# Second norm stage: diagonals of inverse roots made by ScalarE from the identity, VectorE keeps the inverses

## The reference

```
def rms_norm(x, w):
    xf = x.astype(jnp.float32)
    y = xf * lax.rsqrt(jnp.mean(xf * xf, axis=-1, keepdims=True) + EPS)
    return (y * w.astype(jnp.float32)).astype(x.dtype)

def finish(x, y_gla, y_nsa, w_out, norm_mix_post, norm_ffn_pre, norm_ffn_post, w_ff_up, w_ff_down):
    y = jnp.concatenate([y_gla, y_nsa], axis=-1) @ w_out
    x = x + rms_norm(y, norm_mix_post)
    h = rms_norm(x, norm_ffn_pre)
    u = jnp.square(jax.nn.relu(h @ w_ff_up))
    return x + rms_norm(u @ w_ff_down, norm_ffn_post)
```

## Time and profile before

| what | value |
|---|---|
| time, median of 3 runs | 2026.84 us (2023.39 to 2028.88) |
| profiled execution | 2025.4 us, span of its trace 2023.6 us |
| TensorE busy | 1906.8 us (94%) |
| VectorE busy | 689.9 us (34%) |
| GpSimd busy | 547.8 us (27%) |
| ScalarE busy | 519.2 us (26%) |
| second norm stage, in the trace | from 1158.4 us to 1212.1 us |

### The profile page before, as it was taken

How to read it: one execution, slowest core, us unless ns; L and a number is a source line. 1 busy time by engine, 2 the same in 40 slices (tenths; PEclk the granted TensorE clock), 3 DMA queues, 4 the chain that set the end, 5 groups by cost and what they waited for, 6 DMA issues and landing times. The chain is left out here.

```text
span 2023.6 us, 26094 instructions
## 1 busy us (share of the span) xinstructions
PE 1906.8 (94%) x10662; PEld 1550.7 (77%) x10662; DVE 689.9 (34%) x1555; ACT 519.2 (26%) x1169; POOL 547.8 (27%) x458
## 2 busy tenths in 40 slices
PE   7999999879999699999969969999999999999996
PEld 6888887745556487777758768888888888888885
DVE  5321213567665233424230175300332133213323
ACT  3311212377677334334221140010000010000002
POOL 3212222157664221111112143222222222222124
PEclk9999999889999799999969979999999999999998
DMA  4111122120000675656423100111111111111112
GB/s 134 32 52 52 55 51 63 61 89 1 1 1 1 228 239 178 222 181 235 133 60 115 25 21 22 55 48 42 42 42 42 42 42 42 42 42 42 42 53 84
DMA packets 113630, 149.73 MB, mean 74 GB/s; under 512 B 21584, under 2 KB 99320, under 8 KB 105256
## 3 DMA queue, kind: packets, MB, share of 16 engines
q1 hardware_dynamic: 104296, 80.95, 13.3%
q0 software_dynamic: 9216, 67.11, 9.9%
HBM read 139.96 MB, written 12.27 MB: 75 GB/s over the span
## 5 line engine op out<-in xcount | busy, mean ns | idle before, releaser
L278 PE MATMUL PS<-Z,ring 128*128 128x258 f32 x1152 | 258.2, 380 | 0.0
L1816 PE MATMUL PS<-Z 128*128 128x256 f32 (+1 forms) x1024 | 244.6, 385 | 0.0
L278 PEld LDWEIGHTS PS<-Z,ring 128*128 128x128 f32 x1152 | 218.1, 189 | 33.0
L278 PE MATMUL PS<-hT,ring 128*128 128x258 f32 x992 | 226.9, 386 | 7.6 <-DMA ring<-in_w_out 7.0
L1816 PEld LDWEIGHTS PS<-Z 128*128 128x128 f32 x1024 | 186.5, 190 | 42.8 <-issue 20.3
L278 PEld LDWEIGHTS PS<-hT,ring 128*128 128x128 f32 x992 | 190.4, 193 | 37.6 <-DMA ring<-in_w_out 7.1
L2362 ACT ACTIVATE Z<-PS 128x516 f32<-128x516 f32 x80 | 48.1, 601 | 646.9 <-PE PS L278 646.9
L241 POOL TENSOR_TENSOR Z<-ring 128x512 f32<-128x512 f32 x36 | 46.7, 1298 | 604.5 <-PE PS L278 533.5
L278 PE MATMUL PS<-Z 128*128 128x258 f32 x832 | 187.1, 380 | 0.0
L278 PEld LDWEIGHTS PS<-Z 128*128 128x128 f32 x832 | 157.5, 189 | 23.9
L2382 DVE TENSOR_TENSOR Z<-PS,Z 128x516 f32<-128x516 f32 x96 | 66.8, 695 | 314.9 <-PE PS L278 314.9
(11 more groups left out here) (379 smaller groups left out, 2736.7 us busy)
## 6 DMA issues: line engine op xcount, KB each, us to landing
ring<-in_w_ff_up SPq DMA_DIRECT2D x32, 512.0 KB, 5.3
ring<-in_w_ff_down SPq DMA_DIRECT2D x32, 512.0 KB, 4.2
ring<-in_w_in SPq DMA_DIRECT2D x9, 1024.0 KB, 5.0
X<-in_x_prompt SPq DMA_DIRECT2D x8, 1024.0 KB, 11.2
srow<-in_state_nsa_win SPq DMA_DIRECT2D x16, 256.0 KB, 5.3
out_y_prompt<-X SPq DMA_DIRECT2D x8, 512.0 KB
out_win_sample<-in_state_nsa_win SPq DMA_DIRECT2D x1, 4088.0 KB
out_kv_prompt<-Z SPq DMA_DIRECT2D x8, 256.0 KB, 2.0
```

The costliest lines, as they stand in the source:

```text
L278: last = nc.tensor.matmul(M.PS[:, bank_of(M, n, e) + c, 0:CW], a[:, k, :], b[:, k, c * CW:(c + 1) * CW], start=e in (M1, M2, M5) and k == ...
L1816: last = nc.tensor.matmul(out, w1s[:, v, half, 2 * r + e, :], x2[seg][:, r, v, :, e, half:half + SEG[seg]], start=(j == 0), stop=(j == 15))
```

## The change

In the second norm stage (front and back both there) VectorE's `diagonal` now only inverts the root and signals it under a new semaphore, "back_inverse". ScalarE gets a `diagonal` of its own: an ACTIVATE with the function Copy that reads the identity with the inverse root as its scale, and signals "diag_ready". It stands at the start of ScalarE's turn t for tile t - 3, ahead of the square of tile t, and waits for the inverse and, from tile 2 on, for the matmuls of tile t - 2 that read the same buffer. The loop of ScalarE becomes one turn longer. The first and the third norm stage stay as they were.

```
-    rta, rtb = M.sem("front_root"), M.sem("back_root")
+    rta, rtb, invb = M.sem("front_root"), M.sem("back_root"), M.sem("back_inverse")
...
         @block.scalar
         def _(act):
-            for t in range(NT + LAG):
+            def diagonal(t):
+                n = toks(t)
+                act.wait_ge(invb, t + 1)
+                if t >= 2:
+                    act.wait_ge(bkd, b0 + t - 1)
+                nc.scalar.activation(diag[0:n, t % 2, 0:n], M.ident[0:n, 0:n], ACT.Copy, scale=st[0:n, 3, t:t + 1])\
+                  .then_inc(dgr, 1)
+
+            for t in range(NT + PLAG):
+                if front is not None and back is not None and t >= PLAG:
+                    diagonal(t - PLAG)
                 if front is not None and t < NT:
...
-                if back is not None and t >= LAG:
+                if back is not None and LAG <= t < NT + LAG:
...
             def diagonal(t):
                 n = toks(t)
                 dve.wait_ge(rtb, b0 + t + 1)
+                if front is not None:
+                    r = st[0:n, 3, t:t + 1]
+                    nc.vector.reciprocal(r, r).then_inc(invb, 1)
+                    return
                 inverse(t, 2)
```

## The result

| | before | after |
|---|---|---|
| time, median of 4 runs | 2026.63 us (2023.39 to 2028.88) | 2012.31 us (2010.51 to 2014.37) |
| profiled execution, span | 2025.4, 2023.6 us | 2013.24, 2011.5 us |
| second norm stage in the trace | 1158.42 to 1212.05, 53.63 us | 1160.41 to 1199.86, 39.45 us |
| trace behind the stage | 811.55 us | 811.64 us |

The changed kernel is faster: ratio 0.9927, 95% interval 0.9915 to 0.9939, 14.3 us of the medians. The stage is 14.2 us shorter. The spans differ by only 12.1 us, because the stretch ahead of the stage, which the change doesn't touch, took 2.0 us longer in this execution.

A forecast was written before the change was run, and what follows sets the result against it. The prediction took VectorE's move, late behind diagonals held by GpSimd's adds, to bound the second norm stage. Two turns and end piece: 37.35 us before, 14.6 + 10.2 = 24.8 after, gain 12.5, so 2014.3 us, range 2009.5 to 2021.5.

The forecast's parts named there:

- What bounds the stage: Second norm stage: TensorE waits 12.9 us for VectorE's move into hT, late because diagonals of 1649 ns each stand ahead.
- the hold: VectorE's diagonal waits on SBUF ports until GpSimd's add ends: 2.40 us instead of 0.29, 10.9 us over the stage.
- ScalarE's price: Cost of one diagonal as a ScalarE ACTIVATE: 0.39 us, bounded by 0.29 undisturbed and 2.40 if held by the add.
- The turn: Two tiles, from one scaling to the scaling two tiles on: 12.24 us before, 7.29 forecast; two turns 23.53 to 14.6.
- The second ring: ScalarE's and VectorE's chain of waits per tile: 3.35 us, 6.7 a turn, costing nothing until the diagonal passes about 0.7.
- the ring through the move: Chain of scaling, reciprocal, move, matmuls, transposes, square and root back to a scaling: forecast 7.29 us a turn.
- The end piece: From the scaling of tile 8 to the last move: 13.82 us before, forecast 10.2, between 8.6 and 11.8.
- Ahead of tile 4: Stage before the scaling of tile 4: no change, plus or minus 0.7 us, as VectorE's first diagonals met adds only briefly.
- The start of the feed-forward stage: Clock there may be low for longer or shorter than now: no change, plus or minus 1.7 us.
- Rival 1: TensorE's clock stays low: two turns 20.6 us, end 11.8, a gain of 4.9, 2022 us; chance 0.10.
- Rival 2: VectorE's move is held until the add's end instead of the diagonal: gain near 0, 2027 us; chance 0.05.
- Rival 3: ScalarE switches tables, two loads of 1.283 us per diagonal: 2034 us; chance 0.03, shared with a held ScalarE.

The follow-up runs named there:

- e1: Kernel before, VectorE's diagonals in the second norm stage made in the tensor_scalar form that also writes a sum: 2017.55 us, ratio 0.9947.
- e4: Changed kernel, VectorE's move in turns 4 to 8 also waiting for GpSimd's add of the same turn: 2025.75 us, ratio 0.9992.
- e9: Changed kernel with VectorE's move of tile t - 4 at the start of its turn, ahead of the scaling: 2008.82 us (one execution).
- e5: Changed kernel with each of ScalarE's diagonals made twice, the extra one into an unused place: 2014.19 us (one execution).
- e6: Changed kernel with each of ScalarE's diagonals made four times, the extra ones into an unused place: 2019.32 us (one execution).
- e2: Kernel before with VectorE's move of tile t - 4 put ahead of the reciprocal and diagonal of tile t - 2: 2012.26 us (one execution).
- e3: Kernel before with each of GpSimd's adds in the second norm stage made in two halves of 512 columns: 2012.85 us (one execution).
- e8: e7 with VectorE's move of tile t - 5 at the very start of its turn, ahead of the scaling: 2009.13 us, again 2007.44 us.
- e7: Changed kernel with the back half a turn later, move ahead of the reciprocal, ScalarE's diagonal after the front's root: 2009.61 us, ratio 0.9910.

## Why the prediction was right

- **What bounds the stage.** Right, and shown from both sides: e1 takes the hold away and leaves the diagonal where it was, 10.0 of 14.2 us; e4 leaves the diagonal away and puts the old moment of the move back, and the two turns are as long as before.
- **ScalarE's price.** 0.39 us taken, from an Exp of the same shape at another place of the kernel; 0.404 measured, beside the adds too. The upper bound of 2.40 is excluded.
- **The turn.** 7.29 forecast, 7.24 and 7.21 measured. The rows that it was summed from left out that the reciprocal overlaps the move: 0.06 us from one to the other, not 0.19; the matmuls behind a wait took 0.07 more than the rows had.
- **The second ring.** ScalarE's 3.35 us a tile did not bound a turn of the changed kernel, since the ring through the move was longer: the scalings of tiles 4 to 6 are 3.36 and 3.88 us apart, and only the first of these steps is ScalarE's ring. e9 shows it alone, 3.35; e5 and e6 at larger doses, 3.64 and 4.22. That a dearer diagonal costs nothing up to 0.7 us holds for the turns only; ahead of tile 4 and in the end piece e5 paid 0.5 us each.
- **The end piece.** The mis-sized term. I took 10.2 us, midway between 8.6 at full clock and 11.8 at the low one; it was 8.83, at full clock (1.83 us of idle time ahead of it), and 8.84 in both other traces of the changed kernel. This difference is 1.4 of the 1.7 us by which the stage gained more than forecast, and most of the 2 us between 2014.3 and 2012.31. Midway was a choice between two levels, neither of which gives 10.2.
- **Ahead of tile 4.** Taken at nothing with bounds of 0.7 us, and it was 0.1. But the reason given, that the first diagonals met the adds only briefly, holds for that trace and not for the code: in e2, with the same code up to there, both were held whole and the piece took 3.8 us more. That it came out at nothing is partly luck.
- **The start of the feed-forward stage.** Taken at nothing with bounds of 1.7 us: 811.55 and 811.64 us behind the stage, nothing. In five of the other traces (e2, e3, e4, e9 and the first of e8) it is 809.9 to 810.0, so the bound was the right size; the three traces of the changed kernel and the one before all lie on the long side.
- **Rival 1, the low clock,** did not happen in the turns (the blocks took 2.02 us). The argument against it had TensorE's idle time in pieces of about 1 us, which was wrong: they are 1.67 and 0.46 us in the first turn and 0.98 and 0.46 in the second. All three traces of the changed kernel kept the full clock, but e1's first turn, with 2.08 us of idle time, did not, and this cost it 1.67 us.
- **Rival 2, the move takes over the hold,** is excluded: all eight full moves of the changed kernel took 1.19 to 1.22 us, and six of them ran beside adds.
- **Rival 3, table loads,** is excluded: the stage has one load, as before.

## What to carry to other kernels

When one instruction's duration in a trace equals what is left of another engine's instruction at its start, suspect that it is held (e1 and e3 are two ways to show it); its cost is what is queued behind it: here 0.3 us of work delayed the move by 2.3, TensorE's matmuls by as much, and its clock with them. Try first to change the form of the held instruction or its place in the list (10.0 and some 10.6 of the 14.2 us here, the latter counted from tile 4 on) and only then its engine. After such a repair, write down the next rings with their lengths: 7.24 and 6.70 us a turn lay so close that one more line (a move at the start of its turn) gave 1.9 us, and both orders together 4. Compare a stage piece by piece, the pieces that the edit can't touch too: here they showed that 3.8 us of e2 and 0.9 of e5 were not the edit's.

## What the runs showed of the hardware

- VectorE's plain tensor_scalar from SBUF to SBUF is held for the whole of a GpSimd tensor_tensor (2.40 us beside an add of 2.35, 1.32 beside a half of 1.26), while the form that also writes a sum takes 0.35 us beside the same add, at a price of 0.07 us over the undisturbed 0.28 and a second record of 0.08. This agrees with the Trainium skill ("SBUF — State Buffer", section "Who interferes with whom"), which excepts that form.
- After 2.08 us of idle time TensorE's clock fell in e1's first turn and not in the next; e2 and e7 kept it at full through 2.50 and 2.51 us (blocks of 2.05 and 2.02 us). So the idle time just ahead of a block doesn't tell its clock. What does tell it is open. At the start of the feed-forward stage, 0.5 us after the stage's end, the clock differs too. The first five us there in the changed kernel and in e8:

```profile
1200.36:1205.36 5.00, 5.00 (x16) 4.07 (x16) 4.97 (x2) 0.00 (x0) 4.92 (x3) 0.66 0.02 5
```

```profile
1195.88:1200.88 5.00, 5.00 (x24) 4.34 (x24) 4.97 (x2) 0.60 (x1) 4.92 (x3) 1.00 0.00 2
```

The first has a clock of 0.66 and 16 matmuls, the second 1.00 and 24. The stretch behind the stage is 811.6 us in the one and 809.9 in the other: 1.7 us that depend on nothing in the code there, and that e8 gained in one trace and not in its second (811.65).
